# The last two experts interleaved, the last layer two by halves of its outputs, the final norm's weights spread by outer products

## The reference, cut to what matters

```
t = rmsnorm(x, norm_moe)                       # 256 tokens x 1024
combine = top-4 of 32 experts, softmax weights
for w1, b1, w2, b2, ce in experts:             # 32, one after the other
    u = t @ w1 + b1                            # 1024 -> 2048
    g = min(u[:, :1024], 7);  lin = clip(u[:, 1024:], -7, 7)
    a = g * sigmoid(1.702 * g) * (lin + 1)
    y = a @ w2 + b2                            # 1024 -> 1024
    acc = acc + ce[:, None] * y
x = x + acc
out = rmsnorm(x, norm_final)                   # x * rsqrt(mean(x*x) + eps) * norm_final
```

## Time and profile before

| | |
|---|---|
| median of 3 runs (lowest, highest) | 1327.95 us (1327.43, 1328.49) |
| the profiled execution | 1328.85 us, its span 1326.9 us |
| granted TensorE clock | 0.998 of full speed |
| PE busy | 1291.2 us, 97% |
| DVE, ACT busy | 412.7 us (31%), 323.4 us (24%) |
| DMA | 475 MB, 358 GB/s over the span, 429 to 433 GB/s in most slices from 400 us on |
| PE idle before line 1753, by the page | 20.5 us, of it 19.5 us put down to DMAs of `w_exp_in` |
| chain that ended last | PE 75%, DMA 22% |

### The profile page before, as it was taken

The page is one execution under the profiler, slowest core; times in us unless marked ns, Lnnn a source line. Parts: engine busy times, 40 slices in busy tenths (PEclk is TensorE's granted clock), DMA queues, the critical chain, the costliest instruction groups (busy, mean ns, idle before and its releaser), DMA issues.

```text
span 1326.9 us, 15133 instructions
## 1 busy us (share of the span) xinstructions
PE 1291.2 (97%) x6183; PEld 659.7 (50%) x6183; DVE 412.7 (31%) x736; ACT 323.4 (24%) x499; POOL 29.4 (2%) x42
## 2 busy tenths in 40 slices
PE   8999999999999999999999999999999999999997
PEld 8888888888887333333333333333333333333332
DVE  6864665545565121111211121111121111112112
ACT  5665555654444010100101010100011001001012
POOL 4000000000102000000000000000000000000000
PEclk9999999999999999999999999999999999999999
DMA  9553453536679999999999999999999999999996
GB/s 325 193 188 132 186 177 141 204 115 259 206 294 432 428 431 429 432 432 430 432 431 432 431 431 432 431 431 431 433 431 431 431 431 432 429 432 431 430 430 266
DMA packets 68030, 475.12 MB, mean 358 GB/s; under 512 B 7504, under 2 KB 9616, under 8 KB 43408
## 3 DMA queue, kind: packets, MB, share of 16 engines
q1 hardware_dynamic: 65840, 473.28, 85.9%
q10 hardware_dynamic: 2144, 1.21, 0.3%
HBM read 473.42 MB, written 1.05 MB: 358 GB/s over the span
## 4 chain that ended last, share of the span: by engine, by line
PE 75%; DMA 22%; DVE 1%; ACT 1%; issue 1%; SPq 0%; POOL 0%; DVEq 0%; ACTq 0%; POOLq 0%
PE bank L1753 37%; DMA place<-in_w_exp_in 22%; PE bank L1562 18%; PE bank L1541 4%; PE bank L1871 4%; PE bank L1542 2%; PE bank L1549 1%; PE bank L1836 1%; PE bank L1766 1%; PE bank L1776 1%; PE bank L1754 1%; DMA ring<-in_w_in 1%; PE bank L1685 1%; PE bank L1704 1%; PE bank L1812 1%
## 5 line engine op out<-in xcount | busy, mean ns | idle before, releaser
L1753 PE MATMUL bank<-place,fxqT 128*64 128x512 f32 x1520 | 677.5, 596 | 20.5 <-DMA place<-in_w_exp_in 19.5
L1754 PE MATMUL bank<-place,fxqT 128*64 128x512 f32 x1520 | 677.8, 596 | 0.0
L1753 PEld LDWEIGHTS bank<-place,fxqT 128*64 128x64 f32 x1520 | 198.3, 137 | 429.1 <-issue 389.1
L1754 PEld LDWEIGHTS bank<-place,fxqT 128*64 128x64 f32 x1520 | 198.3, 137 | 0.0
L1024 DVE TENSOR_TENSOR w_lo<-ring,w_hi 128x2048 fp32r<-128x2048 f32 x63 | 145.2, 2305 | 103.1 <-ACT w_hi L689 102.9
L689 ACT ACTIVATE w_hi<-ring 128x2048 fp32r<-128x2048 f32 x63 | 120.8, 1917 | 117.0 <-PE bank L1562 105.2
L1361 DVE TENSOR_SCALAR bank<-bank 128x512 f32<-128x512 f32 x32 | 22.4, 700 | 391.6 <-PE bank L1754 391.6
L1562 PE MATMUL bank<-w_hi,h_cat 128*128 128x512 f32 x448 | 141.1, 391 | 0.0
L933 ACT ACTIVATE fxqT<-bank 128x512 f32<-128x512 f32 x32 | 19.1, 598 | 414.1 <-DVE bank L1361 414.1
L1562 PEld LDWEIGHTS bank<-w_hi,h_cat 128*128 128x128 f32 x448 | 84.1, 188 | 17.4
L1352 DVE TENSOR_TENSOR fxqT<-bank,g_rows 128x256 f32<-128x256 f32 x64 | 24.2, 420 | 216.0 <-PE bank L1766 216.0
(11 more groups left out here) (291 smaller groups left out, 1065.5 us busy)
## 6 DMA issues: line engine op xcount, KB each, us to landing
place<-in_w_exp_in SPq DMA_DIRECT2D x125, 2048.0 KB, 36.7
place<-in_w_exp_out SPq DMA_DIRECT2D x63, 2048.0 KB, 37.6
ring<-in_w_in SPq DMA_DIRECT2D x19, 2048.0 KB, 7.5
ring<-in_w_branch SPq DMA_DIRECT2D x6, 2048.0 KB, 7.7
ring<-in_w_mem_kv SPq DMA_DIRECT2D x4, 2048.0 KB, 7.7
ring<-in_w_out SPq DMA_DIRECT2D x2, 2048.0 KB, 11.1
spare<-in_w_exp_in SPq DMA_DIRECT2D x2, 2048.0 KB, 12.2
ring<-in_w_in SPq DMA_DIRECT2D x2, 1024.0 KB, 8.2
```

The costliest lines, as they stand in the source:

```text
L1753: mm(o[0:CAP, :], lhsT, low, start=start, stop=stop)
L1754: return mm(o[CAP:P, :], lhsT, high, start=start, stop=stop)
```

## The change

- **Order of the last two experts.** The pieces are loaded and used as: layer one of expert 30, layer one of expert 31, layer two of 30, layer two of 31 (`LAST_ORDER`, `last_two`).
- **Layer two of expert 31 by output halves.** Its pieces are loaded as `out0` and `out1` of columns 0 to 511, then `out0`, then `out1` in two parts, of columns 512 to 1023. Two `chunk`s are summed for each half, one in bank LINEAR and one in GATE, in products 256 columns wide. Each half is copied by itself (`yS_late`) and added to the sums by `put_late`, with a wait between its two pairs of products. The half biases are plain float32 products.
- **The final norm.** `norm_final` comes as one row (4 KB) into a spare place, and a product of a row of ones with each half of it, in experts 27 and 28, spreads it over 128 partitions; VectorE copies it out of PSUM. TensorE waits for each copy.
- **The end.** Squares of the first 512 columns, the products of these columns with `gfin`, and the mean's first part come before the last `put_late`. After it two squares (512 wide) run on ScalarE beside two products with `gfin` on VectorE. The results are then multiplied by the reciprocal deviation in SBUF, three quarters on VectorE, one on ScalarE.

```diff
+LAST_ORDER = [(NE - 2 + n // W1, n % W1) for n in range(2 * W1)] + [(NE - 2 + n // W2, W1 + n % W2) for n in range(2 * W2)]
+GFIN_AT = (LOOPED * TURN + 2, LOOPED * TURN + 3)
@@ SP
-                sp.dma_start(gfin, norm_final.partition_broadcast(P)).then_inc(loaded, 16)
+                sp.dma_start(gfin_row, norm_final.rearrange("(a n) -> a n", a=1)).then_inc(gfin_in, 16)
...
+                for j in range(W2):
+                    load_chunk(j, 0, slice(0, 4), place_in[late_turn(r, NE - 1, W1 + j)[0]])
+                load_chunk(0, 1, slice(0, 4), late_in[0])
+                for n in range(2):
+                    load_chunk(1, 1, slice(2 * n, 2 * n + 2), late_in[1 + n])
@@ TensorE, experts 27 and 28, between the transposes of the activations and the biases
+                if isinstance(e, int) and e in GFIN_AT:
...
+                    mm(bank[RESULT][:, :], ones_row, gfin_row[:, 512 * h:512 * (h + 1)], start=True, stop=True).then_inc(gfin_turned, 1)
+                    pe.wait_ge(gfin_kept, r * 2 + (h + 1))
@@ TensorE, last two experts
+                layer_one(n, lambda j: late_turn(r, e, j))
+                pe.wait_ge(selWT_ready, n + 1)
+                gather(n * 2 + 4)
+                put(n)
+                turn_gathered(n + 2, RESULT)
+                pe.wait_ge(act_ready, n + 1)
+                turn_acts(acts, TURNS)
+                add_biases(r, n + 1)
+                pe.wait_ge(gotT_ready, (n + 2) * 2)
+                add_late_bias(r, n)
+                layer_one(n + 1, lambda j: late_turn(r, e + 1, j))
+                pe.wait_ge(aT_ready, n + 1)
+                layer_two(0, *late_turn(r, e, W1))
+                turn_weighted(r, n)
+                pe.wait_ge(act_ready, n + 2)
+                turn_acts(acts_late, GATE)
+                pe.wait_ge(pick_out_ready, n + 2)
+                add_half_bias(LINEAR, 0)
+                pe.wait_ge(selWT_ready, n + 2)
+                turn_weighted(r, n + 1)
+                pe.wait_ge(aT_ready, n + 2)
+                add_half_bias(GATE, 1)
+                layer_two(1, *late_turn(r, e, W1 + 1))
...
+                    for k in rows_:
+                        w = place[b][:, k, 512 * h:512 * (h + 1)]
+                        ins = both_halves(o[:, 0:HALF], aT_late[:, k, j, :], w[:, 0:HALF], w[:, HALF:512],
+                                          False, last and k == rows_[-1])
...
+                chunk(bank[LINEAR], b0, 0, range(4), 0, False)
+                put(n + 1)
+                chunk(bank[LINEAR], b1, 1, range(4), 0, True).then_inc(chunk_done, 1)
+                pe.wait_ge(late_in[0], r * 16 + 16)
+                chunk(bank[GATE], b0, 0, range(4), 1, False).then_inc(place_used[b0], 1)
+                put_late(r, 0)
+                for h in range(2):
+                    pe.wait_ge(late_in[1 + h], r * 16 + 16)
+                    ins = chunk(bank[GATE], b1, 1, range(2 * h, 2 * h + 2), 1, h == 1)
+                put_late(r, 1)
@@ put_late
+                for swap in range(2):
+                    if swap:
+                        pe.wait_ge(done, before_ + 2)
                     for t in range(TT):
+                        g = t ^ swap
+                        rows_ = slice(CAP * g, CAP * (g + 1))
+                        mm(sums[:, t, h, HALF * g:HALF * (g + 1)], selWT_late[rows_, t, :], yS_late[rows_, HALF * h:HALF * (h + 1)],
+                           start=False, stop=swap == 1).then_inc(done, 1)
@@ VectorE, the end
+                    dve.wait_ge(put_done, 4 * NE + 4)
+                    keep_scaled(1, 1, final_kept)
+                    dve.wait_ge(final_sq, 1)
+                    keep_scaled(0, 1, final_kept)
...
+                    for j in range(t, 2):
+                        dve.tensor_scalar(results[:, t, cut], results[:, t, cut], rstd[:, t, 0:1], None,
+                                          ALU.mult).then_inc(final_ready, 1)
@@ ScalarE, the end: one square of 512 columns for each t, then std for each t, then
+                act.wait_ge(final_rstd, 2)
+                act.activation(results[:, 1, 0:UW], results[:, 1, 0:UW], ACT.Copy, scale=rstd[:, 1, 0:1]).then_inc(final_scaled, 1)
```

More of the change, by code:

```diff
@@ L418, in for_experts @@
                     expert(r, m, q)
-            for q in range(NE - LOOPED * TURN):
+            for q in range(NE - 2 - LOOPED * TURN):
                 expert(r, LOOPED + q // TURN, q % TURN)
+            last_two(r)
         def moe_turned(q, t):
@@ L464, in load @@
                 dst = place[b][:, :, :].rearrange("p k n -> p (k n)")
[L465 to L475, removed]
+                sp.dma_start(dst, src).then_inc(place_in[b], 16)
             def load_ahead(b):
@@ L1865, in put, with turn_acts, turn_weighted @@
-            def put(k, last=False):
+            def turn_acts(src, b):
+                for g in range(4):
+                    ins = pe.transpose(bank[b][:, P * g:P * (g + 1)], src[:, P * g:P * (g + 1)], ident[:, :])
+                ins.then_inc(act_turned, 1)
+            def turn_weighted(r, n):
+                pe.wait_ge(selW_ready, n * 2 + 2)
+                for t in range(TT):
+                    ins = pe.transpose(bank[TURNS][:, P * t:P * (t + 1)],
+                                       selW[:, t, :, :].rearrange("p o c -> p (o c)"), ident[:, :])
+                ins.then_inc(selT_done, 1)
@@ new lines, in layer_two, with expert @@
+            def layer_two(j, b, used):
+                pe.wait_ge(place_in[b], used * 16 + 16)
+                for k in range(4):
+                    w = place[b][:, k, :]
+                    ins = both_halves(bank[RESULT], aT[:, k, j, :], w[:, 0:512], w[:, 512:D], False,
+                                      j == W2 - 1 and k == 3)
+                ins.then_inc(place_used[b], 1)
+            def expert(r, m, q):
+                e = m * TURN + q
+                n = r * NE + e
+                layer_one(n, lambda j: piece_turn(r, m, PIECES * q + j))
+                pe.wait_ge(selWT_ready, n + 1)
+                gather(n * 2 + 4)
+                put(n)
+                if isinstance(r, int) and isinstance(e, int) and e == LOOPED * TURN:
+                    add_tokens()
+                pe.wait_ge(act_ready, n + 1)
+                pe.wait_ge(got_ready, n + 2)
+                turn_acts(acts, TURNS)
+                if isinstance(e, int) and e in GFIN_AT:
+                    h = GFIN_AT.index(e)
+                    pe.wait_ge(ones_row_ready, r + 1)
+                    pe.wait_ge(gfin_in, r * 16 + 16)
+                    mm(bank[RESULT][:, :], ones_row, gfin_row[:, 512 * h:512 * (h + 1)], start=True, stop=True).then_inc(gfin_turned, 1)
[3 more added lines that the diff above has]
+                pe.wait_ge(aT_ready, n + 1)
+                layer_two(0, *piece_turn(r, m, PIECES * q + W1))
+                turn_gathered(n + 2)
+                layer_two(1, *piece_turn(r, m, PIECES * q + W1 + 1))
+                pe.wait_ge(gotT_ready, (n + 2) * 2)
+                turn_weighted(r, n)
@@ L1867, in put @@
+            def put(k):
                 pe.wait_ge(selWT_ready, k + 1)
@@ L1870, in put @@
                     t, half = q // 2, slice(CAP * (q % 2), CAP * (q % 2 + 1))
-                    mm(bank[SUMS + q][:, :], selWT[half, t, :], yS[half, :], start=False, stop=last).then_inc(put_done, 1)
+                    mm(bank[SUMS + q][:, :], selWT[half, t, :], yS[half, :], start=False, stop=False).then_inc(put_done, 1)
             def add_tokens():
@@ L1890, in experts @@
             def experts(r):
-                for_experts(pe, r, expert)
-                put((r + 1) * NE + r, last=True)
+                for_experts(pe, r, expert, last_two)
             for_rounds(pe, first_tokens, experts, read_late=True)
```

327 lines of the change are left out of this document (182 added, 145 removed).

## The result

The changed kernel takes 1333.52 us (median of 5 runs, 1333.22 to 1335.29), the kernel before 1327.85 beside it. The ratio is 1.0041, interval 1.0029 to 1.0054: slower by 0.4%, where no change was forecast. The forecast time was 1329.35 with a range to 1331.4, so the result lies above the range too. Three of the five executions took 1333.2 to 1333.5, two 1335.1 to 1335.3. The profiled execution took 1333.22, its span is 1331.3 (before: 1328.85 and 1326.9).

The account below looks back on a forecast made before the run. TensorE's queue behind the weights landing at 1298.6, then the tail, bounds the kernel. Last chunk ending 1318.5 to 1319.6 plus 9.2 of tail gives plus 0.8 to 1.9; middle 1.4 makes 1329.35 us, range 1325.9 to 1331.4.

Parts of the forecast that it names:

- The queue from `out0` of expert 30 on: TensorE's work from layer two of expert 30 through the last chunk: 19.8 us, 2.4 more than before.
- From the gather to `out0`: TensorE's work from expert 30's gather to its layer two, with layer one of expert 31: 19.6 us.
- The chunk pairs: Products 256 wide in expert 31's layer two: 0.215 us a pair, 1.8 a chunk with its switch.
- rival (a): Narrow pairs in four chunks and two half biases are bound by issue: 2.0 us more at 0.27 a pair, 1331.3; 15%.
- (b): Weight stream binds at the end: median 1327.1 with landing at 1315.8 (13%), 1324.7 with landing at 1313.4 (10%).
- (c): Short rows slower than in the mixing part: at 260 GB/s last landing 1319.7, median 1331.0; 5%.
- The 2 KB rows: Last 4.19 MB of weights: 345 GB/s against 426, landing at 1315.8, the loss hidden by TensorE's queue.
- the landing of the last store: End of the kernel: 3.36 us from the last store's issue to the end of the span.
- the middle that I took: Stalls reach the end as 0 to 1.1 us, span plus 0.8 to plus 1.9; plus 1.4 was taken.
- the tail: From the last chunk's end to the span's end: 9.2 us against 10.8, a gain of 1.6, bounds 1.0 to 2.2.
- The stall of the outer products: TensorE in experts 27 and 28: 1.8 us each, 3.6 together, after taking off 0.1 for the `aT` wait.
- The cover: Slack of 1.3 us in expert 30 hides part of the outer products' stalls, leaving TensorE 2.3 us late.

Follow-up runs that it names:

- e3: Changed kernel with the next layer one's two bias products moved between the outer product and the wait for its copy; 1330.97 us (ratio 1.0019).
- e9: Changed kernel with the outer product over 128 rows (row 0 ones, the others zeros), same place and wait; 1331.57 us (ratio 1.0021).
- e1: Changed kernel without the outer products, norm_final coming by a broadcasting DMA behind the last weights; 1330.73 us (ratio 1.0016).
- e4: Changed kernel with the fourth quarter of the result stored by SyncE, not ScalarE; 1333.76 us (ratio 1.0041).
- e13: Changed kernel without the two stores of tokens 0 to 127, all computing kept; 1334.14 us (ratio 1.0041).
- e8: Kernel before with only the end recast, on whole blocks, norm_final by DMA, all stores by SyncE; 1328.5 us (ratio 1.0).
- e10: Kernel before with the puts of experts 29 and 30 moved into weight waits, expert 31's first output block loaded in two parts; 1329.12 us (ratio 1.0012).
- e2: Kernel before with only the row, the two outer products and their copies added in experts 27 and 28; 1331.94 us (ratio 1.0026).

## Why the prediction was wrong

The path was the right one, and most of its terms hold. The queue from `out0` of expert 30 on was put at 19.8 us and is 19.76. From the gather to `out0` it was 19.6 and is 19.5. The chunk pairs stand 0.215 apart, as the row of the mixing part had it; rival (a) falls. TensorE's chain in experts 27 to 31 has no wait for weights. Rivals (b) and (c) fall together: the stream is empty by about 1312, 8 us before the last chunk is through. The 2 KB rows run at 408 GB/s at a share of 1.05, against 430. That is 5%, and not the 19% that I took from a window half idle. The 5% that the prediction worked out, as an estimate, from about 3 bus cycles a packet in the Trainium skill (DMA: Bandwidth & Descriptors, section Why small descriptors are slow) agrees with the trace.

Two steps failed: the half clock, which was put at nothing, and the landing of the last store, which was put at 3.36 us. The medians of forecast and result are 4.2 us apart (1329.35 and 1333.52). So are the profiled executions, counted from the `put` of expert 27: the forecast had 130.9 us to the end of the span, its middle, and 135.1 are measured. Of this 1.8 to 2.0 are stalls and clock (points 1 and 2), 0.5 is the middle that I took (point 3), 1.8 the tail (point 4).

1. **The stall of the outer products** was put at 1.8 us each. From the product to the next bias it is 1.90, as computed. But the 0.1 that I took off for `aT` is not there, and the switch to the product adds 0.2: 2.04 each, 0.5 more in all.
2. **The half clock** was put at nothing, neither in the sum nor among the rivals: it is 1.6 us in the profiled execution. I counted the product as time of TensorE and not as one row followed by idle time. Waits for weights of 1.1 us before, at a clock of 1.00, gave no warning; e3 and e9 show that one row and a wait together do it. Both misses, 2.1 us, arrive in expert 30: its gather starts 84.8 us behind the `put` of expert 27, where 82.8 were forecast (1280.15 less 1197.34). The cover was right: the delays of both experts are 5.7 us, 4.3 arrive, so 1.35 are hidden, and 1.3 was forecast.
3. **The middle.** I put the effect of the stalls at the end between nothing and 1.1 us and took half, since the one-row product had no row of its own. They arrive in full, and that half was 0.5.
4. **The tail** was put at 9.2 and is 11.0. The step that failed in it is "from the last store's issue to the end of the span 3.36 us": it is 5.1 (1326.20 to 1331.3). The computing before it is 5.9 (1320.28 to 1326.20), and 5.8 to 6.0 was forecast. e1, e4 and e13 show that the landing goes with neither the outer products, nor the issuer, nor the number of stores; the instruction load beside it is the likely cause and not shown.

From the execution to the median I took off 0.9, since the profiled execution of before was that much above its median. That was right: it was late as a whole ahead of every edit. The one after was not late there, and is 0.3 below its median.

The sign would have been "slower" by the tail alone. Without outer products, and so without points 1 to 3, e1 is 2.6 us above before. Counted from the `put` of expert 27 (1196.66 there), its last chunk ends 2.5 us later than the last product before (121.2 against 118.8), and the tail is 0.1 longer. The forecast had 2.4 for the longer queue, which is right, and paid for it with a tail that gains 1.6. The computing does gain 1.5: 7.4 us before, 5.9 in e1 and after. But the landing takes it back. Without that gain no "same" was left.

## What to carry to other kernels

A `put` or other filler between two dependent steps is cover: before it is moved, look up which engine's chain it hides. A product of one row followed by a wait had a second price here besides its duration, the clock of what comes after it; full rows, or work put behind it, took that price away. A tail is as long as its last store's landing, so keep a wide bound on that term, and look at what else moves on the DMA queues then. And compare two traces by distances from a point ahead of every edit: by the clock of the span alone e8 and e10 looked 0.8 and 0.3 us earlier, where one is 0.3 and the other 0.9 us later.

## What the hardware showed that I had not expected

- A float32 product of 1x128 by 1x512 followed by 0.8 us of idle time brings the granted clock from 1.00 to 0.50 for 3.4 us, in the midst of TensorE at full work, in one (after, e13) or both (e2, e4) of two experts. The same with 128 rows keeps 1.00 (e9); so does the one-row product with 0.1 us of idle time behind it (e3), and 1.84 us of idle time behind full products (e10).
- From the last store's issue (256 KB) to the end of the span it is 3.1 to 4.1 us in the kernels with the old layer two and 4.6 to 5.3 in those with the halved one, with the last 33 KB or so of the stores on about one DMA engine (e13). Neither the issuing engine (e4) nor half of the stored data (e13) changes that. In all seven of the latter, and in none of the former, an instruction packet of 16 KB, 0.9 to 2.0 us long, begins behind that issue.
- Rows of 2 KB cost the DMA engines 5% of their rate (408 against 430 GB/s).
